# Rebuilding the front of a transformer block's attention: weights split in the projection, grouped-query blocks first, the first block's maxima in the expansion, and two scratch layouts turned

## The chip, the cores and the metric

The kernel runs on one core of one Trainium2 chip. The metric is the device time of one execution in microseconds. The time of the kernel before is 3362.53 us, the median of 3 runs (3361.41 to 3363.61).

## What is computed

One layer of a hybrid transformer block over 2048 latent tokens of width 1024 with a prefix of 256 context tokens:

```python
mx = (silu(c) @ w_ada + b_ada)                 # six modulations of 1024
h = (x * (1 + mx[1]) + mx[0]) @ w_in           # one projection for three head groups
# A: 6 latent-attention (MLA) heads, q and kv expanded from ranks 256 and 128, head width 64+32
kv = rms_norm(c_kv) @ w_ukv;  q = rms_norm(c_q) @ w_uq;  rope on 32 of the 96
# B: 6 grouped-query (GQA) heads over 2 kv heads, width 64, rms-normed q and k, rope
# C: gated convolution of width 3 over 256 channels
s = q @ k.T * dq ** -0.5;  o = softmax(s) @ v  # 2048 queries, 2304 keys, both kinds
y = concat(mla, gqa, conv) @ w_o
x = layer_norm(ALPHA * x + mx[2] * y)
y = square(relu((x * (1 + mx[4]) + mx[3]) @ w_mlp1)) @ w_mlp2     # width 4096 inside
out = layer_norm(ALPHA * x + mx[5] * y)
```

All is float32. A product is made of three TensorE products of a high and a low part of each operand (high times high, high times low, low times high), in a rounded float32 type that the profile prints as f32 or fp32r. ScalarE makes a high part by a copy, VectorE the low part by a subtraction.

## The kernel before

The program is a row of stages with a barrier between any two: `stage_modulate`, `stage_project`, `stage_expand`, `stage_attend`, `stage_mix` and `stage_mlp`. Each stage gives each engine a fixed list of instructions, so the order is written by hand, and engines wait for each other at counters only. DMAs are issued by SyncE (SP), in `stage_mix` by ScalarE (ACT) too. What a stage leaves to the next is stored in DRAM scratch tensors (names that begin with s_) and loaded again.

**Projection** takes 18 tiles of 128 tokens; per tile a `split`, the matmuls (L473) and an `out` of copies (L320, L332 to L338). **Expansion** (`stage_expand`) first loads the weights w_ukv and w_uq (L544, L545), splits them (ACT L595, L596, DVE L619, L620), and then makes queries, keys and values of all MLA heads in four blocks of 512 tokens (PE L668), which SP stores. Beside that, it makes 8 of the modulation columns (40 to 47): two loads of w_ada, 2 MB each (`e_wa`), 16 strip matmuls L713, 8 turns L699.

**Attention** (`stage_attend`) has 24 blocks of 1024 queries: for each of 6 heads two MLA blocks, then two GQA blocks. A block goes through 18 key tiles: scores (L1098; six matmuls of 512 columns for MLA, four for GQA, per key tile), ACT's exponentials (L964), and after each sixth key tile the value matmuls (L1111). The softmax subtracts a row maximum that is found one block ahead: 40 items per block (8 query tiles by 5 key chunks, four of 512 keys and one of 256), each one matmul on high parts (L1073) into one of two PSUM banks `a_mx` and one VectorE `reduce_max` (L983), so that PE may issue item c only after the reading of item c-2. `items_of(kt)` gives each key tile of block b two or three items of block b+1, the first behind the first half of the scores and the others behind the second half. After the last key tile, `columns` joins the maxima (L988), negates them into a column of the tile `mcol` (L992), and PE's `lay_row` (L1079, 8 matmuls) turns them to a row that ACT copies into the queries' tile (L942, L944). The 40 items of block 0 stand alone ahead of the first scores. In the first block of each head, four modulation columns are made (8 strip matmuls L713 and 4 turns L1136). VectorE and GpSimd (POOL) sum the exponentials (L1007, L928, L933), and POOL does the convolution.

**Mix** (`stage_mix`) takes 16 tiles of 128 tokens through w_o (PE L1454), layer norm and the right-hand operands of the first MLP product, which go to the scratch `s_uc`. ACT loads the two parts of the attention's output, tile by tile, from `s_mix` (L1315), laid out [part, 8 row groups, 128 partitions, 2048 tokens], and x (L1321).

**MLP** (`stage_mlp`) is a block-recursive product. Its first phase is 2688 matmuls at L2100. Its second (L2108, 2688 too) is two halves (hf) of seven products in `ORDER2`, each of 8 chunks; a chunk's operand is loaded, for some products summed by POOL (L2042, `chunk_sum`), and split (ACT L1751, L1757, DVE L1888, L1890). At the boundary of the halves, `FINISH` closes the first half's layer norm (DVE L2007, POOL's `bias` L2070) while the second half has begun.

## Time and profile before

| what | value |
|---|---|
| median of 3 runs | 3362.53 us |
| profiled execution: its time, its span | 3365.77 us, 3364.0 us |
| mean granted TensorE clock | 0.959 |
| expansion | 441.66 to 540.74 us |
| attention | 540.74 to 1825.91 us |
| mix | 1825.91 to about 2077 us |
| MLP, first and second phase | 2078.8 to 2705 us, 2705.6 to 3340 us |
| VectorE's tail behind PE's last matmul | 3340 to 3364 us |
| busy share of the span: PE, DVE, ACT, POOL | 93%, 70%, 41%, 43% |

The stages follow each other, so the times of their parts that no other engine covers add up to the span. PE is busy through most of it; what is left are stage borders and short waits inside the stages, and those are read stage by stage. A matmul's own duration in the records overlaps the next one's, so a matmul's cost is read from the distance of two starts.

### The profile page before, as it was taken

Reading aid. Unit: us, or ns where it says so; the run is one execution under the profiler, and the core shown is the slowest. Engines: PE = TensorE matmul, PEld = TensorE weight load, DVE = VectorE, ACT = ScalarE, POOL = GpSimd, SP = SyncE. Lnnn points to the kernel's source line nnn. Section 1 sums busy time; section 2 is a strip of 40 time slices with the busy share of each in tenths; the row PEclk is TensorE's granted clock in tenths of the full one; section 3 lists DMA queues with packets and bytes.
Section 4 is the critical chain, followed back from the end, with each engine's and each line's share of the span. In section 5 each row is a group of like instructions: output and inputs, shape, how many; then the busy total and the mean of one; then the engine's idle time right before and its main releaser. Section 6 shows DMA issues by size and latency. Waiting matters only on the chain. (4 is left out here: it accounts for less than half of the span.)

```text
span 3364.0 us, 38645 instructions
## 1 busy us (share of the span) xinstructions
PE 3123.6 (93%) x13713; PEld 2282.1 (68%) x13713; DVE 2344.1 (70%) x3232; ACT 1362.6 (41%) x1930; POOL 1462.9 (43%) x857
## 2 busy tenths in 40 slices
PE   6999955999999999999997987999999999998996
PEld 3888843655555555565654765888788888887885
DVE  4444435677776877767674787778778768887878
ACT  3222221343443434434443334555555544334432
POOL 1233200756657656556563344433333323444443
PEclk8999976999999999999998998999999999999998
DMA  6122289032124222132213777644734388777873
GB/s 236 56 86 86 78 282 273 18 85 60 50 60 97 65 54 65 32 85 53 54 38 94 225 238 267 218 150 160 285 140 159 127 313 295 285 259 270 298 291 143
DMA packets 284043, 515.49 MB, mean 153 GB/s; under 512 B 35872, under 2 KB 158112, under 8 KB 271648
## 3 DMA queue, kind: packets, MB, share of 16 engines
q1 hardware_dynamic: 246560, 475.54, 43.1%
q10 hardware_dynamic: 37312, 37.75, 3.5%
q8 instruction: 98, 1.61, 0.2%
q14 instruction: 73, 0.60, 0.1%
HBM read 356.64 MB, written 156.57 MB: 153 GB/s over the span
## 5 line engine op out<-in xcount | busy, mean ns | idle before, releaser
L983 DVE TENSOR_REDUCE a_mpart<-a_mx 128x1 f32<-128x512 f32 (+1 forms) x960 | 592.5, 635 | 319.6 <-PE a_mx L1073 308.6
L928 POOL TENSOR_TENSOR a_acc_p<-a_acc_p,a_pf 128x1024 f32<-128x1024 f32 x240 | 580.2, 2418 | 229.8 <-ACT a_pf L964 208.1
L964 ACT ACTIVATE a_pf<-a_sc 128x1024 f32<-128x1024 f32 x432 | 441.2, 1024 | 467.7 <-PE a_sc L1098 466.5
L2100 PE MATMUL f_bank<-slot_hi,f_wx 128*128 128x512 f32 x1792 | 557.7, 392 | 15.3 <-DMA slot_lo<-s_uc 8.2
L2100 PEld LDWEIGHTS f_bank<-slot_hi,f_wx 128*128 128x128 f32 x1792 | 339.4, 189 | 88.9 <-DMA slot_lo<-s_uc 10.1
L1111 PE MATMUL a_o<-a_pf,a_v 128*64 128x512 f32 x1728 | 393.1, 605 | 0.0
L2033 POOL TENSOR_TENSOR f_work<-raw_rows 128x512 f32<-128x512 f32 x160 | 220.7, 1381 | 372.4 <-DVE f_wx L1883 368.8
L2108 PE MATMUL f_bank<-slot_hi 128*128 128x512 f32 x896 | 351.3, 392 | 18.4 <-DVE slot_lo L1890 18.4
L2042 POOL TENSOR_TENSOR f_y<-f_y,raw_rows 128x1024 f32<-128x1024 f32 x80 | 219.1, 2740 | 337.1 <-DMA raw_rows<-in_w 337.1
L2100 PE MATMUL f_bank<-slot_lo,f_wx 128*128 128x512 f32 x896 | 351.2, 392 | 0.0
L2108 PE MATMUL f_bank<-slot_lo,slot_hi 128*128 128x512 f32 x896 | 350.5, 391 | 0.0
L2108 PE MATMUL f_bank<-slot_hi,slot_lo 128*128 128x512 f32 x896 | 350.4, 391 | 0.0
L1111 PEld LDWEIGHTS a_o<-a_pf,a_v 128*64 128x64 f32 x1728 | 121.3, 139 | 233.0 <-issue 223.3
L1904 DVE TENSOR_TENSOR f_work<-f_work,f_bank 128x512 f32<-128x512 f32 x256 | 174.3, 681 | 135.6 <-ACT f_work L1773 124.5
L1888 DVE TENSOR_TENSOR slot_lo<-raw_rows,slot_hi 128x1024 fp32r<-128x1024 f32 x112 | 204.4, 1825 | 35.6 <-ACT slot_hi L1751 35.2
L1890 DVE TENSOR_TENSOR slot_lo<-f_y,slot_hi 128x1024 fp32r<-128x1024 f32 x112 | 160.4, 1432 | 97.4 <-ACT slot_hi L1757 96.0
L1073 PE MATMUL a_mx<-a_mk_hi,a_mq_hi 96*128 96x512 f32 (+1 forms) x480 | 193.4, 421 | 33.8 <-DMA a_mq_hi<-s_qr 25.5
L1757 ACT ACTIVATE slot_hi<-f_y 128x1024 fp32r<-128x1024 f32 x112 | 118.8, 1060 | 260.4 <-POOL f_y L2042 253.7
L473 PE MATMUL p_main<-win_hi,u_hi 128*128 128x512 f32 (+2 forms) x528 | 198.2, 375 | 20.0 <-POOL u_lo L416 19.3
L2108 PEld LDWEIGHTS f_bank<-slot_hi 128*128 128x128 f32 x896 | 169.3, 189 | 55.9 <-DVE slot_lo L1890 21.1
L473 PE MATMUL p_main<-win_lo,u_hi 128*128 128x512 f32 (+2 forms) x528 | 196.2, 372 | 0.0
L473 PE MATMUL p_main<-win_hi,u_lo 128*128 128x512 f32 (+2 forms) x528 | 196.1, 371 | 0.0
(278 smaller groups left out, 5862.3 us busy)
## 6 DMA issues: line engine op xcount, KB each, us to landing
raw_rows<-s_hx SPq DMA_DIRECT2D x112, 512.0 KB, 4.3
f_y<-in_w SPq DMA_DIRECT2D x112, 512.0 KB, 5.3
raw_rows<-in_w SPq DMA_DIRECT2D x80, 512.0 KB, 5.9
raw_rows<-in_w SPq DMA_DIRECT2D x32, 1024.0 KB, 4.8
s_hx<-stream SPq DMA_DIRECT2D x128, 256.0 KB, 2.7
s_hx<-f_work SPq DMA_DIRECT2D x96, 256.0 KB, 2.0
a_wa<-in_w_ada SPq DMA_DIRECT2D x6, 2048.0 KB, 9.3
s_uc<-o_ring_hi SPq DMA_DIRECT2D x37, 256.0 KB, 2.9
```

Of the source, the lines that this page charges most:

```text
L473: mm = nc.tensor.matmul(main[:, b, 0:cn], lhs[s][:, k], rhs[:, k, c0:c0 + cn], start=(k == 0 and rhs is w_hi and lhs is u_hi), stop=(k == ...
L928: nc.gpsimd.tensor_tensor(acc[:, :], left[:, :], pf[(b * KT + kt) % NPF][:, :], ALU.add).then_inc(added_p, 1)
L964: nc.scalar.activation(pf[n % NPF][:, :], sc[n % 2][:, :], ACT.Exp, scale=SCALES[0 if is_mla(b) else 1]).then_inc(exped, 1)
L983: nc.vector.reduce_max(mpart[:, s, k:k + 1], mx[c % 2][:, 0:CHUNKS[k][1]], AX.X).then_inc(mx_read, 1)
L1073: nc.tensor.matmul(mx[c % 2][:, 0:width], lhs, rhs, start=True, stop=True).then_inc(mx_done, 1)
L1111: mm = nc.tensor.matmul(o_ps[half * DH:(half + 1) * DH, :], v[0 if is_mla(b) else 1][:, kt], pf[n % NPF][:, half * QB:(half + 1) * QB], st ...
L1888: nc.vector.tensor_tensor(slot_lo[:, s, 0:2, :], x_raw[cc % XN], slot_hi[:, s, 0:2, :], ALU.subtract).then_inc(clo, 1)
L1904: nc.vector.tensor_tensor(t, t, bank[:, (NP * n + pos) % 8, :], plus(sign)).then_inc(c_set, 1)
L2033: nc.gpsimd.tensor_tensor(out, w1_part(n, first), w1_part(n, second), plus(sign)).then_inc(sum_set, 1)
L2042: nc.gpsimd.tensor_tensor(y1[cc % YN], y1[cc % YN], y2[k % Y2N], plus(sign)).then_inc(y_sum, 1)
L2100: mm = nc.tensor.matmul(bank[:, m % 8, :], w[:, k], x[:, s, k, :], start=(k == 0 and j == 0), stop=(k == 3 and j == 2))
L2108: mm = nc.tensor.matmul(bank[:, 4 * (pr % 2) + tt, :], x[:, s, f, tok], y[:, s, 2 + f, :], start=(start and j == 0), stop=(stop and j == 2))
```

## The change

1. **Weights of the expansion.** `stage_project` loads w_ukv and w_uq on SP ahead of its last two tiles and splits them in a new `between()` (3 ACT copies and 3 DVE subtractions of 768, 640 and 640 columns) before the last tile's matmuls are copied out. They stand in a shared tile `low`, which later stages use for other tiles.
2. **Expansion.** The modulations are gone from it. `load_heads(0)` loads the first GQA head's seven operands here, and the 40 items of the first block (now a GQA block) run here: 24 between the products and 16 alone at the end. The rope products stand ahead of the key products.
3. **Attention.** The two GQA blocks of a head come before its two MLA blocks. No items stand ahead of the first scores. Block b runs 36 items when it is GQA and 44 when it is MLA (the first 14 more), counted over all blocks instead of block by block, and placed evenly between the score matmuls. `columns` is one `reduce_max` straight into `mcol`, done when the last item of a block is read, and the sign is in the matrix that `lay_row` multiplies by. Eight blocks instead of six make modulation columns.
4. **Layouts.** `s_mix` is laid out tile by tile: the mix's load of a part is 4 KB in one piece per partition in place of 8 pieces of 512 bytes, and an attention store is in pieces of 512 bytes in place of 2 KB. A store into `s_uc` is one piece of 2 KB per partition in place of four of 512 bytes. The chunks that the first MLP phase multiplies are therefore ordered [partition, j, 512], and the moving operand of each L2100 matmul is four runs of 128 elements, 512 elements apart, in place of one run of 512.
5. **MLP, second phase.** `ORDER2` changes, so that the two products whose second operand needs no POOL sum stand together at the start of a half; the wait for stored results of the first half is split in two, and the last product takes its first two tiles together.

```diff
+                if c == CT + TT - 2:
+                    sp.wait_ge(ulo_set, CT + TT - 1)
+                    for done, (at, w, _, _) in zip(w_up_in, EXPANSION):
+                        sp.dma_start(at, w).then_inc(done, 16)
...
+            def between():
+                for done, (at, _, hi, _) in zip(w_up_in, EXPANSION):
+                    act.wait_ge(done, 16)
+                    nc.scalar.activation(hi, at, ACT.Copy).then_inc(w_up_hi, 1)
...
+        PLACES = [(1, "v")] * VG + [(2, "ring")] * ITEMS + [(2, "v")] * VG + [(3, "ring")] * ITEMS + [(3, "end")] * ALONE
...
+            load_heads(sp, g, 0, heads_in)
...
+            def maxima(items):
+                for c in items:
+                    s, k = MAX_ITEMS[c]
+                    k0, width = MAX_CHUNKS[k]
+                    if c == 0:
+                        pe.wait_ge(heads_in, 16 * LOADS_G)
+                    if c == last_maxima[0]:
+                        pe.wait_ge(v_set, VG * NVG)
+                    need(pe, mx_read, c - 1 if c in last_maxima else c)
+                    nc.tensor.matmul(mx_bank(c)[:, 0:width], g.gq_hl[:, s * P:(s + 1) * P], g.gk_hh[:, k0:k0 + width],
+                                     start=True, stop=True).then_inc(mx_done, 1)
...
-        is_mla = lambda b: b % PER_HEAD < NBLK
+        is_mla = lambda b: b % PER_HEAD >= NBLK
...
+        MOD_BLOCKS = (0, 2, 4, 6, 8, 12, 16, 20)
...
-        items_of = lambda kt: range(NI * kt // (KT - 1), NI * (kt + 1) // (KT - 1)) if kt < KT - 1 else range(0)
+        QUOTA, AHEAD = (36, 36, 44, 44), 14
+        upto = [NI]
+        for b in range(NSB):
+            upto.append(min(upto[-1] + QUOTA[b % PER_HEAD] + (AHEAD if b == 0 else 0), NI * NSB))
+        done_by = lambda b, kt: upto[b] + (upto[b + 1] - upto[b]) * min(kt, KT - 1) // (KT - 1)
...
+                i = head_of(b)
+                if b % PER_HEAD == 0 and i:
+                    sp.wait_ge(pv_done, NBATCH * b)
+                    load_m(i)
+                if b % PER_HEAD == NBLK and i + 1 < HM:
+                    sp.wait_ge(pv_done, NBATCH * b)
+                    load_heads(sp, g, i + 1, in_g)
...
-                dve.wait_ge(mx_read, NI * (b + 1))
-                nc.vector.reduce_max(mneg[:, :], mpart[:, :, :], AX.X).then_inc(max_set, 1)
-                dve.wait_ge(max_set, b + 1)
+                need(dve, mx_read, NI * b)
                 need(dve, row_done, 2 * b)
                 kind, col = (0, QK) if is_mla(b) else (1, DH)
-                nc.vector.tensor_scalar(mcol[kind][:, :, col], mneg[:, :], -1.0, None, ALU.mult).then_inc(col_set, 1)
+                nc.vector.reduce_max(mcol[kind][:, :, col], mpart[b % 2][:, :, :], AX.X).then_inc(col_set, 1)
...
-            for c in range(NI):
-                read_max(0, c)
             columns(0)
...
+                    if half == 1 and m == len(ops) - 1:
+                        mm.then_inc(scored, 1)
+                    at = half * len(ops) + m + 1
+                    for j, c in enumerate(beside):
+                        if at == 2 * len(ops) * (j + 1) // len(beside):
+                            item(c)
...
-                        sp.dma_start(g.mix[part][h // 2][row, cols_of(b, half)], raw(t[half * DH:(half + 1) * DH, :])).then_inc(o_stored, 16)
+                        cols = cols_of(b, half)
+                        tiles = slice(cols.start // P, cols.stop // P)
+                        sp.dma_start(g.mix[part][tiles, row, h // 2, :].rearrange("s p t -> p s t"), by_tile(raw(t[half * DH:(half + 1) * DH, :]))).then_inc(o_stored, 16)
...
-                    act.dma_start(raw(m[s % 2]), g.mix[part][:, :, t * P:(t + 1) * P].rearrange("c p t -> p c t")).then_inc(mix_in[s % 2], 16)
+                    act.dma_start(raw(m[s % 2]), g.mix[part][t]).then_inc(mix_in[s % 2], 16)
...
-                            sp.dma_start(g.uc[p // 4, pos, part][:, :, (p % 4) * P:(p % 4 + 1) * P], by_tile(raw(at[use % RING]))).then_inc(uc_stored[use % RING], 32 // 2)
+                            sp.dma_start(g.uc[p // 4, pos, part][:, p % 4, :], raw(at[use % RING])).then_inc(uc_stored[use % RING], 32 // 2)
...
-        ORDER2 = (5, 3, 2, 4, 1, 6, 7)
+        ORDER2 = (2, 5, 4, 3, 1, 6, 7)
...
-                            mm = nc.tensor.matmul(bank[:, m % 8, :], w[:, k], x[:, s, k, :], start=(k == 0 and j == 0), stop=(k == 3 and j == 2))
+                            mm = nc.tensor.matmul(by_pair(bank[:, m % 8, :]), w[:, k], x[s][:, :, k * P:(k + 1) * P], start=(k == 0 and j == 0), stop=(k == 3 and j == 2))
...
-    g.mix = dram("s_mix", [2, KD, P, T])
+    g.mix = dram("s_mix", [2, TT, P, KD, P])
```

Where instructions stand is shown at three places, with the before first.

On PE at the start of attention, before the change: the end of block 0's forty items (L1073), the row (L1079) and the first scores (L1098).

```order
L1073 MATMUL a_mx<-a_mk_hi,a_mq_hi 128x512 x4
L1073 MATMUL a_mx<-a_mk_hi,a_mq_hi 128x256
L1079 MATMUL a_mx<-ident_r,a_mcol_m 128x128 x8
L1098 MATMUL a_sc<-a_mq_hi,a_mk_hi 128x512
L1098 MATMUL a_sc<-a_mq_lo,a_mk_hi 128x512
L1098 MATMUL a_sc<-a_mq_hi,a_mk_lo 128x512
```

The same place after it; L694 are the last items in the expansion, L1106 the row, L1125 scores, L1099 items.

```order
L694 MATMUL e_v<-h_gk_hh,h_gq_hl 128x512 x4
L694 MATMUL e_v<-h_gk_hh,h_gq_hl 128x256
L520 UNCONDITIONAL_BRANCH
L1080 UNCONDITIONAL_BRANCH
L1106 MATMUL a_mx<-minus_ident_r,low 128x128 x8
L1125 MATMUL a_sc<-h_gq_hl,h_gk_hh 128x512
L1125 MATMUL a_sc<-h_gq_hm,h_gk_lo 128x512
L1099 MATMUL a_mx<-h_gk_hh,h_gq_hl 128x512
```

The forty items have moved across the stage border, and the row comes first in attention.

On VectorE (DVE) in a GQA block before the change, from the sum that closes the block before it to its own end: L983 readings of items, L1007 sums, L1011 and L1016 the normalisation, L988 and L992 the column.

```order
L1011 RECIPROCAL a_rden<-a_t 128x512
L1016 TENSOR_TENSOR a_o_nrm<-a_o_sb,a_rden 128x512
L983 TENSOR_REDUCE a_mpart<-a_mx 128x1 x2
L1021 TENSOR_TENSOR a_o_lo<-a_o_nrm,a_o_hi 128x512
L983 TENSOR_REDUCE a_mpart<-a_mx 128x1 x12
L1007 TENSOR_TENSOR a_acc_d<-a_pf 128x1024
L1007 TENSOR_TENSOR a_acc_d<-a_acc_d,a_pf 128x1024
L983 TENSOR_REDUCE a_mpart<-a_mx 128x1 x12
L988 TENSOR_REDUCE a_mneg<-a_mpart 128x8
L992 TENSOR_SCALAR a_mcol_g<-a_mneg 128x8
L1007 TENSOR_TENSOR a_acc_d<-a_acc_d,a_pf 128x1024 x3
```

And in a GQA block after it: L1013 readings, L1020 the column, L1035 sums.

```order
L1039 RECIPROCAL a_rden<-a_t 128x512
L1044 TENSOR_TENSOR a_o_nrm<-a_o_sb,a_rden 128x512
L1013 TENSOR_REDUCE h_mpart<-a_mx 128x1 x2
L1049 TENSOR_TENSOR low<-a_o_nrm,low 128x512
L1013 TENSOR_REDUCE h_mpart<-a_mx 128x1 x11
L1035 TENSOR_TENSOR a_acc_d<-a_pf 128x1024
L1035 TENSOR_TENSOR a_acc_d<-a_acc_d,a_pf 128x1024
L1013 TENSOR_REDUCE h_mpart<-a_mx 128x1 x5
L1020 TENSOR_REDUCE low<-h_mpart 128x8
L1013 TENSOR_REDUCE h_mpart<-a_mx 128x1 x6
L1035 TENSOR_TENSOR a_acc_d<-a_acc_d,a_pf 128x1024 x3
```

The column has moved from behind the last reading to between readings.

On POOL at the boundary of the second phase's halves before the change: L2042 sums of a chunk, L2070 the bias of the first half's results.

```order
L2042 TENSOR_TENSOR f_y<-f_y,raw_rows 128x1024 x40
L2070 TENSOR_TENSOR f_work<-f_work,f_ln_b 128x1024 x2
L2070 TENSOR_TENSOR stream<-stream,f_ln_b 128x1024 x2
L2042 TENSOR_TENSOR f_y<-f_y,raw_rows 128x1024 x2
L2070 TENSOR_TENSOR f_work<-f_work,f_ln_b 128x1024 x2
L2042 TENSOR_TENSOR f_y<-f_y,raw_rows 128x1024
L2070 TENSOR_TENSOR f_work<-f_work,f_ln_b 128x1024 x2
L2042 TENSOR_TENSOR f_y<-f_y,raw_rows 128x1024 x37
```

And after it (L2072 the sums, L2100 the bias):

```order
L2072 TENSOR_TENSOR f_y<-f_y,raw_rows 128x1024 x40
L2100 TENSOR_TENSOR f_work<-f_work,f_ln_b 128x1024 x2
L2100 TENSOR_TENSOR stream<-stream,f_ln_b 128x1024 x2
L2100 TENSOR_TENSOR f_work<-f_work,f_ln_b 128x1024 x4
L2072 TENSOR_TENSOR f_y<-f_y,raw_rows 128x1024 x40
```

The bias operations of the first half no longer stand between chunk sums of the second.

## Rows read from the trace of the kernel before

**Rows 1.** Windows of two stages: us, busy us by engine (x count), PEclk, DMA share, GB/s.

```profile
586.30:1813.90 1227.60, 1203.47 (x5228) 708.91 (x5228) 883.71 (x1167) 495.15 (x526) 762.35 (x355) 0.99 0.24 57
2078.80:2705.00 626.20, 618.03 (x2698) 509.80 (x2699) 487.10 (x643) 357.27 (x613) 225.91 (x164) 0.99 0.50 188
```

**Rows 2.** PE's groups in the attention body, by shape.

```profile
L1111 PE MATMUL a_o<-a_pf,a_v 128*64 128x512 f32 x1728 | 393.1, 605 | 0.0
L1098 PE MATMUL a_sc<-a_gq_hl,a_gk_hh 128*128 128x512 f32 x432 | 176.1, 408 | 1.2 <-ACT a_pf L964 1.2
...
L713 PE MATMUL a_t<-a_wa,cond_pad 128*32 128x512 f32 x96 | 11.5, 598 | 0.0
```

**Rows 3.** Timeline: projection's end, expansion's start; start, us, instruction, [idle <-releaser].

```profile
417.14 0.60 ACT L320 ACTIVATE h<-p_main 128x512 f32<-128x512 f32 x1 [1.30 <-PE p_main L473]
...
446.62 0.84 ACT L595 ACTIVATE e_ukv_hi<-e_raw_kv 128x768 fp32r<-128x768 f32 x1 [14.88 <-DMA e_raw_q<-in_w_uq]
...
451.07 0.58 PE L668 MATMUL e_ring<-e_ckv_hi,e_ukv_hi 128*128 128x256 f32 x1 [21.54 <-DVE e_uq_lo L620]
```

**Rows 4.** The expansion: its middle window; a DMA issue's KB and us to landing.

```profile
460.00:530.00 70.00, 52.24 (x236) 40.50 (x234) 34.76 (x52) 23.48 (x42) 0.00 (x0) 0.90 1.04 382
...
e_wa<-in_w_ada SPq DMA_DIRECT2D x2, 2048.0 KB, 16.1
```

**Rows 5.** Timeline of DVE and PE, attention's start to its first scores.

```profile
546.03 1.98 DVE L977 MEMSET a_gk_lo<- 1x2304 f32 x1 [0.52 <-issue]
...
552.63 1.19 PE L1073 MATMUL a_mx<-a_mk_hi,a_mq_hi 96*128 96x512 f32 x2 [25.47 <-DMA a_mq_hi<-s_qr]
...
583.64 1.97 PE L1079 MATMUL a_mx<-ident_r,a_mcol_m 128*128 128x128 f32 x8 [0.96 <-DVE a_mcol_m L992]
586.29 0.79 PE L1098 MATMUL a_sc<-a_mq_hi,a_mk_hi 97*128 97x512 f32 x1 [0.68 <-ACT a_mq_hi L942]
```

**Rows 6.** Timeline: PE and DVE around a GQA block's scores, and values.

```profile
918.83 0.50 PE L1098 MATMUL a_sc<-a_gq_hl,a_gk_hh 128*128 128x512 f32 x1
...
921.38 0.39 PE L1073 MATMUL a_mx<-a_gk_hh,a_gq_hl 128*128 128x512 f32 x1
921.72 0.50 PE L1098 MATMUL a_sc<-a_gq_hl,a_gk_hh 128*128 128x512 f32 x1
...
928.75 1.08 PE L1111 MATMUL a_o<-a_pf,a_v 128*64 128x512 f32 x4
...
924.19 3.13 DVE L983 TENSOR_REDUCE a_mpart<-a_mx 128x1 f32<-128x512 f32 x5 [0.26 <-PE a_mx L1073]
...
944.14 1.11 PE L1079 MATMUL a_mx<-ident_r,a_mcol_g 128*128 128x128 f32 x8 [0.93 <-DVE a_mcol_g L992]
...
1793.15 5.37 PE L1111 MATMUL a_o<-a_pf,a_v 128*64 128x512 f32 x24
```

**Rows 7.** PE and ACT, end of attention to the mix's first work.

```profile
1813.95 1.85 PE L1121 MATMUL a_t<-a_acc_p,ones_f 128*64 128x512 f32 x4 [3.41 <-POOL a_acc_p L933]
...
1833.49 3.90 ACT L1328 ACTIVATE slot_hi<-raw_rows 128x1024 fp32r<-128x1024 f32 x4 [12.89 <-issue]
```

**Rows 8.** Mix: PE's groups; DMA issues with KB and us to landing.

```profile
L1454 PE MATMUL o_y<-slot_hi 128*128 128x512 f32 x254 | 83.8, 413 | 15.3 <-DMA slot_lo<-s_mix 15.3
...
L1463 PE MATMUL o_t_x<-ident,o_r 128*128 128x128 f32 x128 | 18.6, 292 | 17.0 <-DVE o_r L1403 17.0
...
o_x<-in_x ACTq DMA_DIRECT2D x14, 512.0 KB, 3.7
...
slot_lo<-s_mix ACTq DMA_DIRECT2D x14, 512.0 KB, 6.3
```

**Rows 9.** POOL and PE at the boundary of MLP's second phase.

```profile
3069.80 6.59 POOL L2070 TENSOR_TENSOR f_work<-f_work,f_ln_b 128x1024 f32<-128x1024 f32 x2 [3.56 <-DVE f_work L2007]
...
3068.64 0.50 PE L2108 MATMUL f_bank<-slot_hi 128*128 128x512 f32 x1 [3.68 <-DVE slot_lo L1890]
...
3082.13 0.79 PE L2108 MATMUL f_bank<-slot_hi 128*128 128x512 f32 x1 [7.75 <-DVE slot_lo L1890]
```

347 lines of the change are left out of this document (173 added, 174 removed).

## The prediction

> **What bounds the kernel now.** I read the windows by stage first, then PE's groups inside a stage, then the timeline at the places where PE's groups have idle time. PE sets the time in both long stages: in the first phase of MLP 2688 matmuls take 626.2 us, 0.233 us each, with all waits in it, and the attention body (first scores to the end of the last block) holds 1227.6 us [rows 1]. How much of the body is work? Counting PE's instructions by group [rows 2]: 2160 score matmuls (five groups of 432 like the one shown), 23 blocks' items (736 of 512 columns at 0.233 us, 184 of 256 columns at half of that), 1728 value matmuls at 0.22 us (24 of them stand in 5.37 us [rows 6]), rows, denominators and six sets of modulation columns for some 60 us together, and the last wait for POOL of 3.4 us [rows 7]. That is 503 + 172 + 22 + 380 + 60 + 3 = 1140 us, so about 86 us of the body are short stops of PE. One shows what they are: from 918.83 to 928.75 a GQA block runs 24 score matmuls and 13 items, whose pure time is 8.4 us, in 9.9 us; in its slow middle the starts are 0.34 us apart (921.38, 921.72) where 0.233 is possible, while VectorE reads maxima without a gap, 5 in 3.13 us, 0.62 us each [rows 6]. PE can't issue item c before the reading of c-2, and VectorE needs 0.62 times 13.3 = 8.3 us for a stretch in which PE has 8.4 us of work, and starts late by its normalisation. Three such stretches give a GQA block about 4.3 us of stops; the last one adds 0.93 us before the row [rows 6]. In an MLA block, PE has 11.5 us per stretch, and the stops are about 2.1 us.
>
> The rest is borders. The expansion starts with a wait for its weights and their splits, and PE's first product is at 451.07 [rows 3]. Its middle is bound by DMA, with a share of 1.04 and 382 GB/s [rows 4]. Attention's first scores come at 586.29, 45.5 us behind the border at 540.74, and most of this is the load of MLA's head and forty items at 0.75 us each (552.63 to 582.7) [rows 5]. In mix, PE waits 15.3 us for `slot_lo` from `s_mix` [rows 8]. In the second MLP phase it stops for 3.68 and 7.75 us behind POOL's two bias operations of 6.59 us [rows 9].
>
> **Part by part.**
>
> Projection. ACT's three copies (2048 columns, 2.1 us at the rate of 0.84 us for 768 [rows 3]) stand ahead of the last tile's copies, where ACT now waits 1.30 us for PE [rows 3]. So +1 us; bounds 0 and, if the weights land late, +4.
>
> Expansion. The start loses the weight load and the splits. From ACT's split at 446.62 to PE's start at 451.07 there are 4.5 us [rows 3], and the inputs, issued right behind the weights, are in at about 446: -5 us if all moved with it. But the body is DMA's: 4 MB of `e_wa` go, and 3.9 MB of head loads come; 1 MB of weights leaves, 2.7 us at 382 GB/s [rows 4]. The 24 items between products are hidden by that bound. The 16 alone cost 12 us at 0.75 us each [rows 5], after PE's last product at about 527; that ends at 539, under the landing of the last stores, which now set the border at 540.74. I take -3 us, and for the bounds -8 and +6: the cover is thin, and each us of delay in the products moves the items past it.
>
> Attention's front. After the border come the four memsets of VectorE, to 548.01, the join of the maxima (0.2 us), and then what now lies between the row at 583.64 and the scores at 586.29, 2.65 us [rows 5]. That is 10.3 us in place of 45.5: -35. The operands are already there. Bounds -37 and -28 (if a first use of the head loads or the constants is late).
>
> Attention's body. Score matmuls, values and the number of items in it (920) don't change. GQA blocks go from 40 to 36 items, so VectorE has 7.4 us of readings for 8.2 us of PE's per stretch instead of 8.3 for 8.4; MLA blocks take the 4, and have room (9.1 for 11.5). The wait for the column (0.93 us at a GQA block's end [rows 6], about 11 us over all blocks) goes, since the column is ready some key tiles earlier. What stays is the late start of VectorE in each stretch. I take the stops from 4.3 to 2.4 us in GQA blocks and from 2.1 to 1.0 in MLA blocks: 12 x 1.9 + 12 x 1.1 = -36, and -5 for the spacing of the items between single matmuls, which ends the pairs issued back to back. The bounds are 0 and -83 (all stops gone). Two more blocks make modulation columns; 16 strips of 0.12 us in spacing (a group of 96 has 11.5 us busy [rows 2]) and their turns are 2.3 us each: +4.6. The last block becomes an MLA block without items; VectorE and POOL will be no later there than now: +1. Body: -35.
>
> Border to mix. ACT issues six DMAs ahead of its first copy, 7.6 us, 12.89 us idle [rows 7]. Contiguous loads are quicker to issue; the copy moves forward: -4, bounds 0 and -6.
>
> Mix. An operand of 512 KB in contiguous rows lands in 3.7 us (`o_x`), and `slot_lo` in pieces of 512 bytes in 6.3 us [rows 8]. Both parts together gain about 4 us per tile, nearly all of each of the six waits (largest 4.2). From 15.3 us I take -13; the next late one is VectorE (`o_r`, 17.0 us already [rows 8]), so the bounds are -4 and -20. The Trainium skill, "DMA: Bandwidth & Descriptors", section Specifications, gives 512 bytes as the smallest transfer that reaches line rate. By that rule the old pieces were already large enough, the new layout would bring nothing, and the sum would end 13 us higher; the landing times of rows 8 speak against it.
>
> Stores of attention in pieces of 512 bytes in place of 2 KB: at a DMA share of 0.24 [rows 1] they are hidden. Without that cover they would be late for the mix only at the last block.
>
> MLP, first phase. The moving operand in four runs: no row shows such an operand of a full matmul. Nearest are rows whose operand is one run, 0.233 us. I take 0; from below nothing can be gained, from above see the rivals.
>
> MLP, second phase. The sums of the second half's first products stand behind POOL's bias operations; with two products that need no sum in front, POOL gets their time as slack (634 us for 14 products, some 45 us each). The two waits (11.4 us) go, and the half clock behind the second (its first matmul lasts 0.79 us against 0.50 behind the first [rows 9]): -13, bounds -4 and -14. VectorE has products 4 and 3 one after the other now, each nearly full; if it falls behind, the gain shrinks. The last product's new order is 0: VectorE's tail of four tiles ends the program, and PE is done 24 us before.
>
> Sum: +1 - 3 - 35 - 35 - 4 - 13 - 13 = -102. The profiled execution of before took 3365.77 us (its span 3364.0), 3.2 us above the median, so the profiled one would be 3264 and the median **3260 us**, 3.1% less.
>
> **Rivals.**
>
> *VectorE stays the pacer of the body.* If the stops come from its late start in a stretch, and not from the number of readings, the body keeps its 86 us but for the waits of the row. The item count speaks for my reading, VectorE's gap-free rows at 924.19 for this one. Body -6: 3289 us; with the expansion's tail exposed too, 3300. Chance 0.2.
>
> *All stops vanish.* 12 x 4.3 + 12 x 2.1 and the restarts give -83 for the body's stops, -42 more than mine: 3218 us. Chance 0.08.
>
> *The mix gains nothing*, as VectorE's chain takes each wait over (17.0 us of waits for it show how near it is): 3273 us. This is the time that the skill's rule on 512 bytes would give as well. Chance 0.1.
>
> *Slower: the strided moving operand.* 2688 matmuls in phase 1 read four runs of 128 elements. At 10 ns more each this is +27 us; the gain of 102 is used up at 38 ns each, 16% of 0.233 us, and at twice the time per matmul the kernel would take 3886 us. Against it: runs of 128 elements are long. For it: nothing in the trace shows such an operand. Chance 0.04 beyond that point, and 0.03 for a part of it (same or a little faster).
>
> *The change doesn't do what it says*: the head loads arrive late in the expansion, so PE stands at its first item in block 1 with the products behind it. That costs at most their time, 10 us: 3270. It is inside my forecast, whose own chance is 0.55.
>
> **The range.** The forecast's own bounds reach from 3235 to 3285. To hold 8 in 10 I take in the pacer rival and most of the vanishing stops: 3215 to 3302. What is left out is the slower rival and either end. A measurement of this kernel tells 0.2% from no change. Faster 0.94, within 0.2% 0.02, slower 0.04.
>
> **What would show it.** First scores about 10.3 us behind attention's border; that border near 538; GQA blocks at 44.5 to 45.5 us from row to row in place of 47.4, MLA blocks near 53.4; no VectorE release ahead of `lay_row`; `slot_lo` from `s_mix` landing in under 4.5 us and PE's idle for it under 3 us; phase 1 of MLP at 626 us; no stop over 1 us at the boundary of the halves. I would be wrong first by the body: if blocks keep 47.4 us, or if phase 1 grows.

## The result, and the profile after it

The changed kernel takes 3322.14 us, the median of 4 runs (3315.27 to 3327.66), where the kernel before took 3363.0 us beside it (4 runs, 3361.41 to 3363.61): ratio 0.9873 [0.9857, 0.9888]. It is 1.3% faster, where 3.1% was forecast, and outside the range. The profiled execution took 3320.91 us, with a span of 3319.1 us and a mean granted clock of 0.964.

The span, cut at the same instructions in both traces:

| part | before | after | difference | forecast |
|---|---|---|---|---|
| to the expansion's first load | 441.66 | 441.07 | -0.6 | +1 |
| expansion, to attention's border, 0.3 us ahead of VectorE's first instruction there | 99.1 | 117.9 | **+18.8** | -3 |
| from there to the first scores | 45.5 | 10.3 | -35.3 | -35 |
| body, to the last denominators | 1227.6 | 1198.1 | -29.5 | -35 |
| to the mix's first matmul | 22.0 | 17.5 | -4.5 | -4 |
| mix | 242.9 | 240.8 | **-2.1** | -13 |
| MLP, first phase | 626.8 | 627.4 | +0.6 | 0 |
| MLP, second phase, to the end of the span | 658.4 | 666.1 | **+7.7** | -13 |
| sum | | | -44.9 | -102 |

Three parts went against the forecast. What stands first is what went as forecast. Windows of attention's body and of the first MLP phase after the change, with the columns of [rows 1]:

```profile
569.20:1767.30 1198.10, 1183.89 (x5276) 716.35 (x5276) 888.84 (x1148) 497.57 (x526) 766.42 (x355) 0.99 0.27 66
2025.60:2652.90 627.30, 619.14 (x2703) 510.82 (x2704) 487.13 (x643) 357.75 (x613) 226.06 (x164) 0.99 0.50 188
```

The first phase has 2688 matmuls with the strided moving operand, and its length is that of [rows 1]. The body is shorter. The timeline of DVE and PE from attention's border to its first scores, which answers to [rows 5]:

```profile
559.25 0.91 DVE L1002 MEMSET low<- 128x1024 f32 x1 [0.56 <-PEq L520]
...
566.63 1.94 PE L1106 MATMUL a_mx<-minus_ident_r,low 128*128 128x128 f32 x8 [8.40 <-DVE low L1020]
569.25 0.80 PE L1125 MATMUL a_sc<-h_gq_hl,h_gk_hh 128*128 128x512 f32 x1 [0.68 <-ACT h_gq_hm L972]
```

The row waits for the memsets and the column alone, and the scores come 10.0 us behind the border. But the border itself, 541.02 before, is at 559.25. The timeline of SP's queue, PE and DVE in the expansion shows two causes:

```profile
460.02 0.61 SPq L740 DMA_DIRECT2D h_gv<-s_vg  x1
461.15 18.95 SPq L577 DMA_DIRECT2D s_qn<-e_st_hi  x1
...
487.32 0.76 PE L677 MATMUL e_ring<-e_ckv_hi,low 128*128 128x512 f32 x1 [10.07 <-DVE e_st_lo L633]
...
512.48 0.28 PE L694 MATMUL e_mx<-h_gk_hh,h_gq_hl 128*128 128x256 f32 x1
516.78 0.80 PE L694 MATMUL e_mx<-h_gk_hh,h_gq_hl 128*128 128x512 f32 x1 [3.33 <-DVE h_mpart L639]
...
511.99 0.69 DVE L650 TENSOR_TENSOR e_rt<-e_rope,e_cs 96x512 f32<-96x512 f32 x1 [1.72 <-PE e_rope L677]
515.12 0.68 DVE L656 TENSOR_TENSOR e_ro<-e_rt 96x512 f32<-96x512 f32 x1
516.32 0.41 DVE L639 TENSOR_REDUCE h_mpart<-e_mx 128x1 f32<-128x256 f32 x1
```

First, SP issues the next store behind the seventh head load, and the issue takes 18.95 us. SP issues no other store in that time, and PE then stands for 10.07 us. Second, an item has one bank (`e_mx`). The one of 512.48 is read only at 516.32, since VectorE's rope work of the block stands ahead of the reading. PE stops for 3.33 us and then runs its products 0.43 us apart (517.38, 517.81) in place of 0.23 (512.60, 512.83). DMA, which was to cover all this, in the window of [rows 4] and in a later one that holds the items:

```profile
460.00:530.00 70.00, 48.15 (x174) 36.35 (x174) 35.83 (x55) 19.76 (x37) 0.00 (x0) 0.83 0.99 307
487.00:560.00 73.00, 53.70 (x163) 36.37 (x163) 50.19 (x80) 17.73 (x31) 0.10 (x1) 0.76 0.77 272
```

In the window of [rows 4] the DMA engines are still full (0.99, where it was 1.04), but they move 307 GB/s in place of 382. From 487 on, where the items stand, the share is 0.77, and DMA doesn't cover them.

The mix, PE's groups and DMA issues, with the columns of [rows 8]:

```profile
L1481 PE MATMUL o_y<-low,slot_hi 128*128 128x512 f32 x128 | 44.7, 433 | 15.3 <-DMA slot_lo<-s_mix 15.3
...
L1490 PE MATMUL o_t_x<-ident,o_r 128*128 128x128 f32 x128 | 18.1, 287 | 16.4 <-DVE o_r L1430 16.4
...
slot_lo<-s_mix ACTq DMA_DIRECT2D x14, 512.0 KB, 5.5
```

PE waits 15.3 us for `slot_lo`, as it did before. Of that, 2.2 us stand ahead of the mix's first matmul, which [rows 8] leaves out; from that matmul on it is 13.1 us, and VectorE waits 2.0 us for the same loads, which it didn't before. The second MLP phase: PE's stops (timeline) and the operand that VectorE finishes last.

```profile
3019.38 0.50 PE L2138 MATMUL f_bank<-slot_hi 128*128 128x512 f32 x1 [1.63 <-DVE slot_lo L1920]
...
3152.70 0.50 PE L2138 MATMUL f_bank<-slot_hi 128*128 128x512 f32 x1 [1.79 <-DVE slot_lo L1920]
...
3246.01 0.50 PE L2138 MATMUL f_bank<-slot_hi 128*128 128x512 f32 x1 [2.67 <-DVE slot_lo L1920]
...
3259.55 1.23 DVE L1920 TENSOR_TENSOR slot_lo<-f_y,low 128x1024 fp32r<-128x1024 f32 x1
```

The stops of 3.68 and 7.75 us [rows 9] have become one of 1.63. But there are ten stops of 0.37 to 2.67 us from 3139 on, 14.2 us together, where the kernel before had three late ones (2.78, 3.67 and 0.54 us, from 3296 to 3306). All stops of PE in the phase come to 15.9 us, where they were 18.4.

### The profile page after: what moved, and what is told of

Read it like the earlier page. It is cut to its first block and busy times, and to the rows that moved or that the text cites. A ratio compares the mean times of both kernels' runs of the same rounds, so it can differ in the third digit from the quotient of the medians.

```text
span 3319.1 us, 38700 instructions
## 1 busy us (share of the span) xinstructions
PE 3094.8 (93%) x13713; PEld 2284.4 (69%) x13713; DVE 2353.9 (71%) x3209; ACT 1364.2 (41%) x1931; POOL 1465.9 (44%) x857
## 5 line engine op out<-in xcount | busy, mean ns | idle before, releaser
L1013 DVE TENSOR_REDUCE h_mpart<-a_mx 128x1 f32<-128x512 f32 x920 | 568.4, 636 | 265.2 <-PE a_mx L1099 256.1
L992 ACT ACTIVATE a_pf<-a_sc 128x1024 f32<-128x1024 f32 x432 | 442.9, 1025 | 476.3 <-PE a_sc L1125 471.0
L2130 PE MATMUL f_bank<-slot_hi,f_wx 128*128 128x512 f32 x1280 | 402.6, 392 | 9.0 <-DVE f_wx L1913 7.1
L2072 POOL TENSOR_TENSOR f_y<-f_y,raw_rows 128x1024 f32<-128x1024 f32 x80 | 216.9, 2712 | 331.4 <-DMA raw_rows<-in_w 331.4
L2130 PEld LDWEIGHTS f_bank<-slot_hi,f_wx 128*128 128x128 f32 x1280 | 242.5, 189 | 60.4 <-DVE f_wx L1913 7.5
L2138 PE MATMUL f_bank<-slot_lo,slot_hi 128*128 128x512 f32 x672 | 262.9, 391 | 0.0
L2138 PE MATMUL f_bank<-slot_hi,slot_lo 128*128 128x512 f32 x672 | 262.5, 391 | 0.0
L2130 PEld LDWEIGHTS f_bank<-slot_lo,f_wx 128*128 128x128 f32 x896 | 169.8, 189 | 35.5
L1099 PE MATMUL a_mx<-a_mk_hi,a_mq_hi 96*128 96x512 f32 (+1 forms) x480 | 186.2, 388 | 7.6 <-DVE h_mpart L1013 7.2
L1142 PE MATMUL a_o<-a_pf,h_gv 128*64 128x512 f32 x864 | 192.8, 595 | 0.0
L1142 PE MATMUL a_o<-a_pf,a_v 128*64 128x512 f32 x864 | 192.7, 595 | 0.0
L1125 PE MATMUL a_sc<-h_gq_hl,h_gk_hh 128*128 128x512 f32 x432 | 176.5, 409 | 0.7 <-ACT h_gq_hm L972 0.7
L1125 PE MATMUL a_sc<-a_mq_hi,a_mk_hi 97*128 97x512 f32 x432 | 177.0, 410 | 0.0
```

Source lines behind the costliest of these rows:

```text
L992: nc.scalar.activation(pf[n % NPF][:, :], sc[n % 2][:, :], ACT.Exp, scale=SCALES[0 if is_mla(b) else 1]).then_inc(exped, 1)
L1013: nc.vector.reduce_max(mpart[b % 2][:, s, k:k + 1], mx[c % 2][:, 0:CHUNKS[k][1]], AX.X).then_inc(mx_read, 1)
L1099: nc.tensor.matmul(mx[c % 2][:, 0:width], lhs, rhs, start=True, stop=True).then_inc(mx_done, 1)
L1125: mm = nc.tensor.matmul(out, x, y, start=(m == 0), stop=(m == len(ops) - 1))
L1142: mm = nc.tensor.matmul(o_ps[half * DH:(half + 1) * DH, :], v[0 if is_mla(b) else 1][:, kt], pf[n % NPF][:, half * QB:(half + 1) * QB], st ...
L2072: nc.gpsimd.tensor_tensor(y1[cc % YN], y1[cc % YN], y2[k % Y2N], plus(sign)).then_inc(y_sum, 1)
```

## The experiments

Every edit is made to the changed kernel, and the stages are read at the same instructions as in the table above. "Products" is the start of PE's last product of the expansion (543.5 in the changed kernel), "border" VectorE's first instruction of attention (559.3). Four traces have the expansion exactly as changed (the changed kernel, e4, e9, e11). Their products are at 543.5, 540.5, 540.7 and 543.5 and their borders at 559.3, 556.3, 556.2 and 559.3, so a difference of 3 us in this stage shows nothing. Most kernels have two or three edits, each in a stage of its own, and each is read in its stage; a kernel with one run has no interval.

### e1_gv_late_mix_old

`h_gv`, 576 KB in pieces of 256 bytes, is loaded at attention's start instead of in the expansion; and `s_mix` has its old layout.

```diff
-    sp.dma_start(g.gv[:, :, :], g.vg[:, :, krows]).then_inc(done, 16)
+    if h:
+        sp.dma_start(g.gv[:, :, :], g.vg[:, :, krows]).then_inc(done, 16)
...
-    g.mix = dram("s_mix", [2, TT, P, KD, P])
+    g.mix = dram("s_mix", [2, KD, P, T])
...
-                    act.dma_start(raw(m[s % 2]), g.mix[part][t]).then_inc(mix_in[s % 2], 16)
+                    act.dma_start(raw(m[s % 2]), g.mix[part][:, :, t * P:(t + 1) * P].rearrange("c p t -> p c t")).then_inc(mix_in[s % 2], 16)
```

> Two edits to the changed kernel, in stages that are read apart. (1) Expansion: the load of the first head's values (h_gv, pieces of 256 bytes) is issued at attention's start instead of in the expansion. In the changed kernel the expansion lasts 117.9 us (441.07 to 558.98), SP's next DMA behind h_gv takes 18.95 us to issue, and PE then waits 10.07 us. Theory Q (the small pieces of h_gv clog the queue): the issue takes under 6 us and the expansion shrinks by 8 to 12 us. Rival B (all seven head loads are slow, about 225 GB/s wherever they stand): it shrinks by 1 to 3 us, the share of 576 KB in 3.9 MB. Rival I (the items between products are what costs): no change. (2) Mix: s_mix is laid out as before the change, with loads in pieces of 512 bytes. The mix takes 240.8 us from its first matmul to that of MLP in the changed kernel, 242.9 before. Theory V (VectorE's chain paces mix): unchanged within 3 us. Rival L (the layout gave some us and something else took them): 8 to 13 us longer than 240.8.

One run, 3325.89 us. The issue that took 18.95 us, and PE's wait (timeline of SP's queue and PE):

```profile
461.81 0.37 SPq L577 DMA_DIRECT2D s_qn<-e_st_hi  x1
...
484.14 0.76 PE L677 MATMUL e_ring<-e_ckv_hi,low 128*128 128x512 f32 x1 [6.98 <-DVE e_st_lo L633]
```

Without this load no issue of the expansion takes over 5.26 us. It isn't the only load that an issue can stand behind: at attention's start one takes 11.11 us in the changed kernel, behind the block's first loads and with no `h_gv` ahead of it, and 9.7 to 11.6 us in the others. Products (538.9) and border (554.7) gain 4.6 us against the changed kernel and 1.6 against e4 and e9, which is within the scatter, and PE still waits 6.98 us. So the blocked issue is a small part of what the loads cost. The rest may be that SP's stores share a full DMA with seven loads (the lower GB/s above); no run separates the two. The mix is where the layout is told apart:

```profile
L1483 PE MATMUL o_y<-low,slot_hi 128*128 128x512 f32 x128 | 45.3, 437 | 24.5 <-DMA slot_lo<-s_mix 17.6 <-DVE slot_lo L1400 6.7
...
slot_lo<-s_mix ACTq DMA_DIRECT2D x14, 512.0 KB, 6.4
```

The old layout lands 0.9 us later, and the mix takes 240.5 us with it and 240.8 without: nothing. It costs something ahead of the mix: from the last denominators to the first matmul it is 22.5 us, as before the change, against 17.5. ACT's six issues there (four loads from `s_mix`, two of x) take 8.0 us with the old layout (7.5 in the kernel before) and 2.9 with the new one.

### e2_items_at_end_order_old

All 40 items stand behind the products; and `ORDER2` is the old one, with the tables that belong to it.

```diff
-        ALONE = 16
-        PLACES = [(1, "v")] * VG + [(2, "ring")] * ITEMS + [(2, "v")] * VG + [(3, "ring")] * ITEMS + [(3, "end")] * ALONE
+        ALONE = len(MAX_ITEMS)
+        PLACES = [(3, "end")] * ALONE
...
-        ORDER2 = (2, 5, 4, 3, 1, 6, 7)
+        ORDER2 = (5, 3, 2, 4, 1, 6, 7)
```

> Two edits to the changed kernel. (1) Expansion: all 40 items of the first block stand alone at its end, none between products; the head loads stay where they are. Changed kernel: 117.9 us, of which 12 us are 16 items alone at the end. Rival I (items between products cost time by the single bank's wait for VectorE): the products end 10 us earlier or more, and 24 more items alone take 18 us, so that the stage gets 5 to 10 us longer. Theory Q or B (the loads cost it): the products end within 3 us of now and the stage gets 15 to 18 us longer. (2) MLP's second phase has the old ORDER2 with its tables. Theory O (the new order puts five products with sums in a row, and the chunks fall behind, which delays VectorE's last chunk by 8 us): the stops of 0.4 to 2.7 us from 3139 on vanish, the stop of about 11 us at the boundary of the halves returns, and the time from phase 2's first matmul to the program's end goes from 666.1 us back to 658. Rival T (the last product's tile order costs the 8 us): it stays above 664.

One run, 3320.51 us. Products are at 527.9, 15.6 us earlier than in the changed kernel and 12.6 earlier than in e4: that is what 24 items between the products cost, 0.5 to 0.65 us each, about one reading. The border is 3.9 us later (563.1), as 24 more items stand alone now. PE's stop behind the loads stays (10.50 us). The second phase is 656.7 us to the end, 9.4 less. Of the stops after 3139 two small ones are left (0.75 and 1.88 us, at 3255 and 3260), and one of before is back (PE's timeline):

```profile
3034.72 0.79 PE L2138 MATMUL f_bank<-slot_hi 128*128 128x512 f32 x1 [7.76 <-DVE slot_lo L1920]
```

### e3_heads_late_quota40

As e2 in the expansion; the head loads are issued after its third block; and every block runs 40 items.

```diff
-            load_heads(sp, g, 0, heads_in)
             for b in range(NQB):
...
+                if b == 2:
+                    load_heads(sp, g, 0, heads_in)
...
-        QUOTA, AHEAD = (36, 36, 44, 44), 14
+        QUOTA, AHEAD = (40, 40, 40, 40), 14
```

> Two edits to the changed kernel. (1) Expansion: as in the run with all 40 items at the end, and the seven head loads are issued behind the third block's stores instead of ahead of the first block's. Theory B or Q: the products end 10 to 20 us earlier than in the run with the items at the end and early loads (no issue of 19 us ahead of the first block's stores), and the 40 items follow at once or wait up to 10 us for the loads. Rival I: no difference to that run. (2) Attention: each block runs 40 items (GQA 40, MLA 40) in place of 36 and 44. In the changed kernel GQA blocks take 43.9 us and 46.9 with modulations, MLA 53.2 to 53.8 undisturbed. Theory N (the number of readings per stretch makes VectorE late): GQA blocks take 46 to 47.5 us again, MLA 52.5. Rival P (what helped is that the column no longer ends the block and that items stand apart): GQA 44.9, MLA 52.3, the work of 4 items each way.

One run, 3328.44 us. Products are at 512.4, 15.5 us before those of e2: the price of the early loads. But the border is at 565.4, since the price moved with them (SP's queue and PE):

```profile
515.35 0.60 SPq L741 DMA_DIRECT2D h_gv<-s_vg  x1
515.99 16.41 SPq L577 DMA_DIRECT2D s_qn<-e_st_hi  x1
...
534.33 1.22 PE L695 MATMUL e_v<-h_gk_hh,h_gq_hl 128*128 128x512 f32 x2 [21.58 <-DMA h_gv<-s_vg]
```

Two rows of PE bound a GQA block, here and in the changed kernel:

```profile
830.28 1.08 PE L1107 MATMUL a_mx<-minus_ident_r,low 128*128 128x128 f32 x8
876.57 1.08 PE L1107 MATMUL a_mx<-minus_ident_r,low 128*128 128x128 f32 x8
```

```profile
818.33 1.01 PE L1106 MATMUL a_mx<-minus_ident_r,low 128*128 128x128 f32 x8
862.21 1.08 PE L1106 MATMUL a_mx<-minus_ident_r,low 128*128 128x128 f32 x8
```

46.3 us with 40 items and 43.9 with 36: 0.6 us per item. Of this, 0.233 us is the item's own matmul, and 0.35 us are short stops of PE among scores and items, which grow with the number of items. That is a reading's time, but VectorE isn't full: it is busy for 34.5 of the 43.9 us and for 37.0 of the 46.3. MLA blocks lose 1.6 us (53.6 to 52.0) for four items fewer, 0.4 each.

### e4_items_in_bursts_last_old

Items as before the change, the first behind the first half of a key tile's scores and the rest behind the second, at the new quota; and the last product takes its tiles one by one.

```diff
-                    for j, c in enumerate(beside):
-                        if at == 2 * len(ops) * (j + 1) // len(beside):
-                            item(c)
+                    if m == len(ops) - 1:
+                        for c in (list(beside)[:1], list(beside)[1:])[half]:
+                            item(c)
...
-            for tiles in ((0, 1), (2,), (3,)):
+            for tiles in ((0,), (1,), (2,), (3,)):
```

> Two edits to the changed kernel. (1) Attention: the items stand as before the change, the first behind the first half of a key tile's scores, the others back to back behind the second half; all else as changed. Theory S (even spacing saves PE's waits for readings): MLA blocks get 2 to 3 us longer (they have 2 or 3 items per key tile), GQA blocks stay at 43.9. Rival N (only the count per stretch matters): no block changes by over 0.5 us. (2) MLP: the last product takes its four tiles one after the other as before. Rival T (the new tile order costs the 8 us at the end): the time from phase 2's first matmul to the end falls from 666.1 to 658. Theory O: it stays within 2 us of 666.

One run, 3355.42 us. PE's rows around an MLA block:

```profile
933.73 1.01 PE L1106 MATMUL a_mx<-minus_ident_r,low 128*128 128x128 f32 x8
991.74 1.01 PE L1106 MATMUL a_mx<-minus_ident_r,low 128*128 128x128 f32 x8
```

58.0 us, where the changed kernel has 53.8, and GQA blocks stay at 44.0. The body is 41.6 us longer: the spacing, put down at 5 us, is what lets an MLA block take 44 items at all. The second phase, 663.1 us, is 3 us shorter. Kernels with this `ORDER2` have 663.1 to 666.8 us, so the order of tiles in the last product is worth 3 us at most.

### e5_part_late_conv_gqa_order3

Three of the head loads (`gk_lo`, `gq_hm`, `gv`), which only the scores and values need, go behind the expansion's last stores; the convolution runs in GQA blocks of heads 1 to 4; and products 1 and 3 change places.

```diff
-        part_in = lambda b: head_of(b) * NBLK + b % NBLK if is_mla(b) and head_of(b) * NBLK < len(PARTS) else None
+        part_in = lambda b: (head_of(b) - 1) * NBLK + b % NBLK if not is_mla(b) and 0 <= (head_of(b) - 1) * NBLK < len(PARTS) else None
...
+            load_rest(sp, g, 0, heads_in)
             sp.wait_ge(st_stored[0], 32 * NQB)
...
-        ORDER2 = (2, 5, 4, 3, 1, 6, 7)
+        ORDER2 = (2, 5, 4, 1, 3, 6, 7)
```

> Three edits to the changed kernel, each read in its own stage. (1) Expansion: of the head loads only the four that the items read come early; h_gk_lo, h_gq_hm and h_gv are issued behind the last block's stores. Places of the items as in the changed kernel. By the runs so far (moving h_gv alone gave 4.5 us, moving all gave 15.5 us of the products' time) I expect the last product at 534 to 539 instead of 543.5 and the border at 550 to 555 instead of 559. If it stays at 559, the late loads set the border. (2) Attention: GpSimd's convolution stands in GQA blocks of heads 1 to 4 instead of MLA blocks of heads 0 to 3. Theory C (VectorE's normalisation takes 5.44 us in the third and seventh of these MLA blocks, 1.0 to 1.5 elsewhere, because GpSimd works beside it, and PE stops 2.3 us and then runs slow for some us): no normalisation over 3 us, MLA blocks with modulations at 55.9 and without at 53.8, none at 60; the body gets 8 to 13 us shorter. Rival D (the long normalisation comes from the modulations or a DMA and not from the convolution): blocks of 60 us stay where they are. (3) MLP: ORDER2 = (2, 5, 4, 1, 3, 6, 7), which keeps two products without sums in front but sets product 1 between the two that load VectorE most. Theory A (the lag comes from products 4 and 3 side by side): the stops in the second half go, and phase 2 to the end takes 655 to 659 us instead of 666.1. Theory R (five products with sums in a row are too many whatever their order): it stays above 663.

3311.48 us (3303.41 to 3320.87, 4 runs), ratio 0.9825 [0.9792, 0.9859]. Products are at 530.8 and the border at 550.95, 8.3 us earlier, and set by the late loads now: the items end at 545.5. No MLA block above 55.7 us is left, but two GQA blocks are at 49.5 and 48.4. The second phase is 666.7 us: five products that need POOL's sums still stand in a row, and this exchange among them changes nothing.

### e6_all_end_quota34_mlp_old

Loads as in e5, all 40 items at the end, 34 and 46 items per block, both old orders in the second phase.

```diff
-        QUOTA, AHEAD = (36, 36, 44, 44), 14
+        QUOTA, AHEAD = (34, 34, 46, 46), 14
```

> Three edits to the changed kernel. (1) Expansion: the three loads late as in the run beside this one, and all 40 items alone at the end. The products should end near 519 to 523 (527.9 with all loads early, 512.4 with all late), the items take 30 us more, so the border comes at 554 to 558: about the same as with items between products. If items between products cost nothing in themselves, it would be 10 us later than the run beside it. (2) Attention: quota 34 for GQA and 46 for MLA. From 40/40 to 36/44 a GQA block got 2.3 us shorter and an MLA block 1.8 us longer. If VectorE's readings still pace GQA blocks, they fall by another 1.2 us to 42.7 and MLA rises by 0.9 to 54.7; if GQA is at PE's work already, it falls by 0.5 (2 items at 0.233 us) only. (3) MLP: order and tile order of the last product both as before the change; what stays changed is the split wait for stored results and the ordering of slots. Phase 2 to the end: 656 to 659 us (before 658.4, with the old order alone 656.7).

One run, 3299.27 us. Products are at 516.3, 11.6 us before those of e2, which differs from it in the expansion only by the three late loads; the border is at 551.55. GQA blocks have 42.9 us (0.5 us per item that left). The MLA blocks beside which nothing else runs have 54.2 to 55.4, so a head gains little or nothing by the new quota. The second phase takes 660.6 us, where 656 to 659 were expected.

### e7_best_conv_gqa and e8_best_conv_mla

`gk_lo` and `gq_hm` behind block 2, `gv` behind the last stores; six items between the products of block 3 and 34 at the end, where they rotate over three banks; quota 34 and 46; old `ORDER2`. e7 has the convolution in GQA blocks, e8 leaves it in MLA blocks: the two differ in this alone.

```diff
-        mx_bank = lambda c: v_ps[:, c % 2, :] if c in last_maxima else mx_ps[:, :]
+        mx_bank = lambda c: (v_ps[:, 0, :], v_ps[:, 1, :], mx_ps[:, :])[(c - ITEMS) % 3] if c in last_maxima else mx_ps[:, :]
...
-                    need(pe, mx_read, c - 1 if c in last_maxima else c)
+                    need(pe, mx_read, c - 2 if c in last_maxima and c > last_maxima[0] + 1 else c)
```

> Put together from what the runs showed. Expansion: six of the first block's items between the last block's products and 34 alone at the end in three banks in place of two; h_gk_lo and h_gq_hm loaded behind the third block's stores, h_gv behind the last's. Attention: quota 34 and 46, convolution in GQA blocks. MLP: old ORDER2, new tile order of the last product. Theory: products end near 519, items at 0.62 us each (VectorE's reading, no longer two banks' ping-pong at 0.75) to 541, border at 545 to 548 (559 in the changed kernel, 550.95 with items between the products). Body 1185 to 1192 (1198.1). MLP's second phase to the end 656 to 659 (666.1). Sum 20 to 33 us under the changed kernel: 3290 to 3302 us. If three banks don't help, items still take 0.75 us and the border is at 550.

> The same kernel with the convolution in the MLA blocks, as in the changed kernel. Theory C (GpSimd's convolution beside VectorE's normalisation costs PE 4 to 7 us in single blocks, wherever it stands): the body is within 5 us of that of the run beside it, and the blocks that are over 2 us too long are MLA blocks here (58 to 60 us) and GQA blocks there (48 to 50 us). If MLA blocks in heads 0 to 3 keep 58 us in both, the convolution isn't the cause.

e7 takes 3283.21 us (3278.98 to 3289.34), ratio 0.9763 [0.9736, 0.9789]; e8 3293.36 us (3289.37 to 3295.71), ratio 0.9791 [0.9768, 0.9815]. The runs of the two just don't overlap, and the traces show where the difference arises. The bodies are 1179.7 and 1190.6 us. VectorE's normalisation, in e7 and then in e8:

```profile
873.35 1.50 DVE L1062 TENSOR_TENSOR a_o_nrm<-a_o_sb,a_rden 128x512 f32<-128x512 f32 x1
```

```profile
875.54 5.23 DVE L1062 TENSOR_TENSOR a_o_nrm<-a_o_sb,a_rden 128x512 f32<-128x512 f32 x1
```

In e8 three are this long, and the blocks around them take 59.6, 59.5 and 56.7 us where e7 has 56.1, 56.1 and 53.3: 3.4 us each, 10.3 of the bodies' 10.9. The 34 items take 550.1 - 530.3 = 19.8 us, 0.58 each with three banks where it was 0.75 with two [rows 5]. The six items between products move their end from about 517 to 526.7.

### e9_order_old_only

The old `ORDER2` with its tables, alone.

> The changed kernel with the old ORDER2 and its tables, nothing else. From the run that had this with the items at the end: phase 2 to the end 656.7 us in place of 666.1. Theory O: 656 to 660 here, all other stages within 4 us of the changed kernel, time 3310 to 3318 us. If it is 664 or more, what helped there was chance.

3316.52 us (3307.58 to 3321.94), ratio 0.9868 [0.9844, 0.9892] to a kernel before at 3364.07; the whole is too close to the changed kernel (3322.14, and 3314.12 in e11) to be told apart, so the stage decides. In the profiled execution, the fastest of the four, it takes 654.0 us, 12.1 less than in the changed kernel. The two old stops (2.55 and 7.77 us) are back, and none is later (PE's timeline):

```profile
3027.17 0.79 PE L2138 MATMUL f_bank<-slot_hi 128*128 128x512 f32 x1 [7.77 <-DVE slot_lo L1920]
```

Over all traces, the second phase to the end has 663.1 to 666.8 us with product 2 first (the changed kernel twice, e1, e3, e4, e5) and 654.0 to 662.2 with the old order (before, e2, e6 to e10): no overlap, though the nearest two are 0.9 us apart, and means of 665 and 658. So the order costs about 7 us, and 12 in this trace.

### e10_best_all_end and e11_after_again

e10 is e7 with all 40 items at the end, in three banks. e11 is the changed kernel again, on the same chip.

```diff
-        ALONE = 16
-        PLACES = [(1, "v")] * VG + [(2, "ring")] * ITEMS + [(2, "v")] * VG + [(3, "ring")] * ITEMS + [(3, "end")] * ALONE
+        ALONE = len(MAX_ITEMS)
+        PLACES = [(3, "end")] * ALONE
```

> As the run with the convolution in GQA blocks and all other findings (3283 us), but no item between products: all 40 alone at the expansion's end in three banks. There the six items of the last block delayed the products to 526.7 (516.3 with none), because PE's next item waits until VectorE has done a block's rope and reads the single bank. Theory I: the last product at 515 to 519, first item about 520, 40 readings at 0.58 us, border at 544 to 547 instead of 550.7; all else the same, 3278 to 3281 us. If the late loads set the border instead, it stays at 549 to 551.

> The changed kernel once more, beside the run above on the same chip, for a second trace of it. Expansion 118 us, body 1198 with three or two MLA blocks of 59 to 62 us, phase 2 to the end 663 to 667 us; ratio to the kernel before 0.986 to 0.989. If phase 2 comes out at 658 or less, the effect of the order is within what a single trace scatters.

e10 takes 3280.05 us (3278.59 to 3284.28), ratio 0.9738 [0.9721, 0.9754]; e11 3314.12 us (3299.64 to 3326.31), ratio 0.9827 [0.9788, 0.9865], both to a kernel before at 3369.25. The changed kernel's two medians are 8 us apart and its runs spread over 27 us; e10's lie within 6, and 34 us below e11. e10 is the fastest of all, 2.6% under the kernel before. In e11's trace the body takes 1199.0 us and the second phase 666.8, so the stages are those of the changed kernel. e10's second item and its border (PE and DVE):

```profile
523.06 0.79 PE L697 MATMUL e_v<-h_gk_hh,h_gq_hl 128*128 128x512 f32 x1 [5.13 <-DVE h_mpart L642]
...
546.03 0.91 DVE L1020 MEMSET low<- 128x1024 f32 x1 [0.56 <-PEq L520]
```

Products are at 517.3, and the first item is issued right behind them, at 517.53. The second waits 5.13 us for the reading of the first, ahead of which VectorE's rope work stands. The other 39 run from 523 to 546 at 0.58 us each, in which VectorE reads without a gap. The border is 13.2 us before that of the changed kernel.

## Why the prediction failed, step by step

**Expansion: "The 24 items between products are hidden by that bound", and "4 MB of `e_wa` go, and 3.9 MB of head loads come". Both failed.** +18.8 us where -3 was taken and +6 was the far bound. The first product starts 5.6 us earlier (445.52 for 451.07), as was forecast. The rest is read from the distance between it and the start of the last product:

| kernel | loads and small work beside the products | first to last product |
|---|---|---|
| before | `e_wa`, 8 modulation columns | 74.9 |
| e3 | nothing | 64.4 |
| e2 | head loads | 81.8 |
| changed, e4, e9, e11 | head loads, 24 items | 98.0, 95.1, 94.2, 95.9 |

So the exchange of `e_wa` and its columns for the head loads cost 7 us, where it was to gain 2.7, and the items cost 12 to 16, where they were to cost nothing. The loads were priced by bytes, at the 382 GB/s of the loads that they replaced; the stretch with head loads and stores ran at 307. Against no loads at all they cost 15.5 us at the products (e3 to e2), and three of the seven, late, gave back 11.6 (e6 to e2). How that splits between the blocked issue and the lower rate is open: e1 took away the long issue and gained 1.6 to 4.6 us. The kernel before had a blocked issue in view, in SP's queue at attention's start, behind the same kind of load:

```profile
551.70 0.60 SPq L809 DMA_DIRECT2D a_v<-s_vg  x1
552.34 27.38 SPq L813 DMA_DIRECT2D a_wa<-in_w_ada  x1
```

27.38 us for one issue, and I didn't read it, as nothing waited there for what stood behind. The rival that the loads would be late was named, but priced as "costs at most their time, 10 us": they cost 15 at the products. And the items cost because each waits for a reading out of one bank, with the rope work ahead of that reading. The prediction's own row of the alone items [rows 5] said 0.75 us each, over two banks, and was used only for the 16 at the end. With loads in two parts, all items at the end and three banks, the border is at 546.0 (e10), still 5 us behind the 541.0 of before.

**Attention's front: right**, -35.3 for -35.

**Body: -29.5 for -35. The main term was right in sum, two smaller ones were not.** Short stops and spacing were to give -41, 1.9 us per GQA block and the rest in the MLA blocks. GQA blocks went from 47.4 to 43.9 us and MLA blocks kept their 53.6. The quota moved four items, 0.9 us of PE's own work, from each GQA block to an MLA block. So the stops fell by 2.6 us in a GQA block (1.9 were taken) and by 0.9 in an MLA block (1.1 were taken), -42 over 24 blocks. Without the even spacing the MLA blocks would be at 58 (e4). What was mis-sized is the rest. Modulations cost 3.0 us per block (46.9 against 43.9), in eight blocks, and in the kernel before about 2.2 (55.9 against 53.7), in six: +11 and not +4.6. The first block, with 14 items more, takes 51.2 us (+4), and the last two MLA blocks, with 34 items and with none, 50.5 and 50.9 (-6). Then there are blocks with a long normalisation, 60.1 and 60.3 us (4.1 and 7.2 above the blocks like them), and before the change there were others like them: about +2 in sum. -42, +11, +4, -6 and +2 are -31. VectorE, POOL and PE in the first of these blocks:

```profile
884.81 5.44 DVE L1044 TENSOR_TENSOR a_o_nrm<-a_o_sb,a_rden 128x512 f32<-128x512 f32 x1
...
1089.51 1.02 DVE L1044 TENSOR_TENSOR a_o_nrm<-a_o_sb,a_rden 128x512 f32<-128x512 f32 x1
...
885.10 1.26 POOL L932 TENSOR_TENSOR a_cy<-a_cy,a_ct 128x512 f32<-128x512 f32 x1
886.33 2.38 POOL L956 TENSOR_TENSOR a_acc_p<-a_acc_p,a_pf 128x1024 f32<-128x1024 f32 x1
888.67 1.04 POOL L930 TENSOR_TENSOR a_ct<-a_cp,gcol 128x512 f32<-128x512 f32 x1
...
890.91 0.50 PE L1099 MATMUL a_mx<-a_mk_hi,a_mq_hi 96*128 96x512 f32 x1 [2.33 <-DVE h_mpart L1013]
```

The same instruction takes 0.7 to 2.9 us elsewhere (1.02 in the row shown). Here it begins while a POOL operation is under way and spans the three that follow without a gap, two of the convolution with one of the sums between them, and the next item waits 2.33 us. It ends at 890.25, 0.54 us after the last of them (889.71). In all traces the long ones, 4.6 to 5.5 us, end 0.54 to 0.55 us after such a run of POOL operations; in the kernel before, one ends at 1225.37 behind a run that ends at 1224.82. e7 and e8 show that the place of the convolution decides it, for 10.9 us. The Trainium skill, "SBUF — State Buffer", section "SBUF: two separate sides", says that VectorE with two SBUF inputs and a GpSimd operation that reads SBUF take one shared port pair as an exclusive lock, each for the whole of its instruction. The trace agrees in kind, since the operation that grows has two such inputs; but it shows VectorE waiting through three further GpSimd instructions, where the Trainium skill speaks of one.

**Border to mix: right**, -4.5 for -4; e1 puts it on the layout (22.5 with the old one), where ACT's six issues take 8.0 us in place of 2.9.

**Mix: "Both parts together gain about 4 us per tile" failed**, -2.1 for -13. `o_x` and `slot_lo` are not alike: `slot_lo` is issued behind the others, so its landing counts their bytes too. Its landing went from 6.3 to 5.5 us, a gain of 0.8 us where 2.6 had been read off `o_x`. And PE's wait depends on when it is issued, too. ACT, its queue and PE around one tile:

```profile
1900.59 0.20 ACT L1381 ACTIVATE o_rstd<-o_var 128x1 f32<-128x1 f32 x1 [1.19 <-DVE o_var L1423]
1901.44 0.45 ACTq L1342 DMA_DIRECT2D slot_lo<-s_mix  x1
...
1907.15 1.22 PE L1481 MATMUL o_y<-low,slot_hi 128*128 128x512 f32 x2 [3.40 <-DMA slot_lo<-s_mix]
```

The load is issued by ACT, behind a root that waits for VectorE's statistics. The Trainium skill, "DMA: Bandwidth & Descriptors", section Specifications, puts line rate at transfers of 512 bytes and more, so by it the old pieces needed no mending. The runs agree: 240.5 us with pieces of 512 bytes and 240.8 with 4 KB. The prediction gave this rival 0.1, which was too little against a comparison of unlike loads.

**MLP, first phase: right.** 627.4 for 626.8 us: four runs of 128 elements cost a matmul nothing.

**MLP, second phase: "two products that need no sum in front, POOL gets their time as slack" failed.** +7.7 for -13. The stops at the boundary went as said, so the slack came where it was wanted, but "if it falls behind, the gain shrinks" named the wrong size: it turned the sign. PE reaches the last product 574.2 us after the phase began, where it was 580.4 before, so the gain of the boundary got that far. Then the last product takes 59.8 us, where it was 54.1, for PE waits for its operands, and PE ends where it did (634.0 us for 634.4). The end of the span isn't PE's, though, but that of VectorE's work behind the last operand. Five products with sums now stand in a row, and a chunk goes through loads, POOL, ACT and VectorE. The chain that ended last shows one turn of it:

```profile
3234.24 6.81 DMA raw_rows<-in_w
...
3241.18 2.44 POOL f_y L2072
...
3243.64 1.06 ACT slot_hi L1787
...
3244.73 1.23 DVE slot_lo L1920
3245.95 3.33 DVE slot_lo L1918
```

The last chunk's low part is made at 3259.55, 606.6 us after the phase began; before it was 3304.51 - 2705.64 = 598.9. With the old order it is at 594.4 in e9 and 597.2 in e2. From it to the end of the span there are 59.5 us in all of them, so the 7.7 us go to the end undiminished. That the order is the cause is shown: the old one alone gives 12.1 us back in e9's trace and 7 in the means of all traces, and in e5 an exchange of two among the five changes nothing. That the chain of loads, POOL, ACT and VectorE is too slow over five such products, and why the stops come in the second half alone, are argued from this chain and not shown.

**What the sum would have been.** With +19, -2 and +8 for the three failed steps and the rest as on record, the forecast is +1 + 19 - 35 - 35 - 4 - 2 + 0 + 8 = -48; measured is -44.9.

## What to carry to other kernels

Price a load that is moved into a full stretch by what its queue does behind it, and look for the longest issue behind the same load elsewhere in the trace: bytes at the 382 GB/s of other loads said nothing of an issue of 19 us, or of a stretch that then ran at 307. A stretch that one resource bounds may hide another's work, but here it did not hide a handshake over a single buffer: count the reader's turn, with what stands ahead of it in that engine's list. Before a faster transfer is credited, find what sets the moment of its issue; and when a stop is moved away by giving an engine slack in one place, add up its chain over the stretch from which the slack was taken.

## What the runs showed of the hardware

- One DMA issue of SP took 18.95, 16.41 and 27.38 us when it stood behind the load of a head's values (576 KB in pieces of 256 bytes); with that load gone, the longest of the expansion was 5.26. At attention's start an issue of 9.7 to 11.6 us came without that load ahead of it.
- Six load issues of ACT ahead of the mix, four of them from `s_mix`, took 7.5 and 8.0 us when these four had 8 pieces of 512 bytes per partition, and 2.9 us with one piece of 4 KB, though the stage behind them was no faster (240.5 and 240.8 us).
- A 128x512 VectorE operation with two inputs took 0.7 to 2.9 us, and 4.6 to 5.5 us when a gapless run of POOL operations stood beside it, at whose end it ended too (0.54 to 0.55 us later). Moving POOL's convolution by two blocks was worth 10.9 us.
- Before a stop of 3.33 us the granted clock was 1.00 and PE's starts 0.23 us apart; behind it, from 516.8 to 524, it was 0.50, the lower of the two levels, and they were 0.43 us apart. So a stop can cost more than itself.
- A chain of one matmul and one `reduce_max` per item ran at 0.75 us over two banks and at 0.58 us over three, where VectorE read without a gap.
- A moving operand of four runs of 128 elements, 512 elements apart, was as fast as one run of 512: 2688 matmuls in 627.4 and 626.8 us.
